# A hybrid decoder layer on 8 cores: a second residual tile, the next chunk's LayerNorm prologue placed inside the FFN, and one weight slot less

## The reference

```
x = layer_norm(x)
q, k, v, c_val, c_gate = split(x @ w_in)
att = rms_norm(causal differential attention(q, k, v))          # 4 heads
c = silu(group_norm(causal_conv31(c_val * sigmoid(c_gate)))) @ w_pw + b_pw
x = layer_norm(ALPHA * x + concat(att, c) @ w_o)                 # LN1
x = layer_norm(ALPHA * x + cross_attention(x, mem) @ w_o_mem)    # LN2
h = silu(x @ w_gate) * (x @ w_up)                                # d_ff = 2816
x = layer_norm(ALPHA * x + h @ w_down)                           # LN3, output
```

## Time and profile before

| | |
|---|---|
| runs before | 6143.0, 6189.2 and 6359.51 us; median 6189.2 |
| profiled execution | 6132.52 us, span of its slowest core 6130.7 us |
| spans of the 8 cores | 6099.5 to 6130.7 us |
| mean granted TensorE clock | 0.807 to 0.810 of full speed |
| busy: TensorE, DVE, ACT | 66%, 38%, 39% of the span |
| one chunk of the second phase | some 394 us, eight times |

### The profile page before, as it was taken

One profiled execution on the slowest core, in us unless ns is written; L12 is line 12 of the kernel. 1 busy time (PEld: TensorE's weight loads), 2 busy tenths in 40 slices (PEclk: granted clock), 3 DMA queues, 4 the chain that ended last, 5 costly groups with the idle time before them and its releaser, 6 DMA issues.

```text
span 6130.7 us, 75261 instructions; the slowest of 8 cores (6099.5 to 6130.7 us)
## 1 busy us (share of the span) xinstructions
PE 4025.9 (66%) x24208; PEld 2004.2 (33%) x24208; DVE 2327.8 (38%) x5354; ACT 2396.5 (39%) x3180; POOL 196.2 (3%) x230
## 2 busy tenths in 40 slices
PE   4566776776666767777467575684666846658467
PEld 2333433443333333344223232231322322223223
DVE  3433333122543331321353453535534345244453
ACT  2455665765445556567231221312213113132131
POOL 0000000000000000000001000010000000000000
PEclk8778888887777778888679787796877977879778
DMA  3111111011111100100538255382473743826536
GB/s 84 42 42 42 42 42 42 1 25 42 69 42 42 42 28 15 42 15 1 103 55 130 56 94 112 55 124 65 83 127 57 106 89 62 148 42 102 108 55 107
DMA packets 273353, 395.66 MB, mean 65 GB/s; under 512 B 6964, under 2 KB 230732, under 8 KB 272972
## 3 DMA queue, kind: packets, MB, share of 16 engines
q0 software_dynamic: 226848, 217.07, 23.9%
q1 hardware_dynamic: 46124, 173.77, 8.1%
HBM read 591.09 MB, written 16.78 MB: 99 GB/s over the span
## 4 chain that ended last, share of the span: by engine, by line
PE 41%; ACT 20%; DVE 19%; issue 9%; DMA 9%; DVEq 1%; ACTq 0%; SPq 0%; POOL 0%; POOLq 0%
PE PS L394 39%; ACT U L595 10%; ACT U L388 3%; DVE U L338 3%; DVE U L336 2%; DMA U<-w_up 2%; ACT U L361 2%; DMA U<-xown 2%; DMA U<-xkv 2%; DMA U<-w_down 2%; DVE U L880 2%; PE PS L378 1%; DVEq L148 1%; DVE U L357 1%; DVE U L340 1%
## 5 line engine op out<-in xcount | busy, mean ns | idle before, releaser
L394 PE MATMUL PS<-U 128*128 128x129 bf16 (+4 forms) x21696 | 3720.1, 327 | 780.9 <-ACT U L595 232.7
L394 PEld LDWEIGHTS PS<-U 128*128 128x128 bf16 (+2 forms) x21696 | 1811.2, 104 | 2653.8 <-issue 1719.2
L595 ACT ACTIVATE U<-PS,U 128x1024 bf16<-128x1024 f32 (+3 forms) x1152 | 1163.0, 1041 | 225.5 <-PE PS L394 155.7
L378 PE MATMUL PS<-U 128*128 128x128 bf16 x2368 | 307.7, 269 | 805.8 <-ACT U L361 654.3
L587 DVE TENSOR_TENSOR PS<-PS,U 128x128 f32<-128x128 f32 x512 | 137.9, 296 | 1250.3 <-PE PS L394 1249.1
L378 PEld LDWEIGHTS PS<-U 128*128 128x128 bf16 x2368 | 188.1, 115 | 924.3 <-issue 922.3
L388 ACT ACTIVATE U<-PS,U 128x512 bf16<-128x512 bf16 (+1 forms) x512 | 369.9, 755 | 203.9 <-PE PS L378 199.6
L479 PE MATMUL PS<-U 128*128 128x128 bf16 x128 | 34.0, 265 | 475.9 <-DVE U L477 475.9
L740 DVE SCALAR_TENSOR_TENSOR U<-U,PS 128x512 f32<-128x512 f32 x192 | 132.1, 688 | 481.6 <-PE PS L394 481.6
L908 ACT ACTIVATE U<-PS 128x512 f32<-128x512 f32 x176 | 105.1, 597 | 490.3 <-PE PS L394 431.5
L336 DVE BATCH_NORM_STATS2 U<-U 128x6 f32<-128x512 f32 x328 | 214.5, 654 | 189.6 <-DMA U<-xown 106.7
(11 more groups left out here) (80 smaller groups left out, 1821.9 us busy)
## 6 DMA issues: line engine op xcount, KB each, us to landing
U<-xkv SPq DMA_DIRECT2D x32, 2048.0 KB, 7.6
U<-xown SPq DMA_DIRECT2D x24, 2048.0 KB, 7.7
U<-w_gate POOLq DMA_DIRECT2D x40, 1024.0 KB, 10.4
U<-w_up POOLq DMA_DIRECT2D x40, 1024.0 KB, 13.8
U<-rowp SPq DMA_DIRECT2D x64, 512.0 KB, 6.5
U<-w_down POOLq DMA_DIRECT2D x32, 1024.0 KB, 16.3
U<-w_in POOLq DMA_DIRECT2D x16, 1024.0 KB, 13.9
U<-w_o POOLq DMA_DIRECT2D x16, 1024.0 KB, 8.7
```

Source lines behind the costliest of these rows:

```text
L378: P.op(PE, lambda e, j=j, dt=dt, tpb=tpb, j0=j0, zt=zt: e.transpose(out=tpb[:, (j - j0) * 128:(j - j0 + 1) * 128], in_=zt[:, j, dt * 128:( ...
L394: P.op(PE, lambda e: e.matmul(out, lhsT=lhsT, rhs=rhs, start=start, stop=stop, skip_group_check=True), reads=reads, writes=writes)
L595: P.op(ACT, lambda e, Sps=Sps, pti=pti, q0=q0, bcol=bcol: e.activation(out=Pt[pti][:, :, q0:512], in_=Sps.rearrange("p (a b) -> p a b", a= ...
```

## The change

It does four things.
- `R2`, a second residual tile of 16 KB per partition, is added, and chunks alternate between `R` and `R2`. Room is made by `NSLOT` 3 instead of 4 (8 KB per partition), by laying `xh32` over the two `sg` tiles (`sgx`), and by laying `memT` into `hT`.
- The prologue becomes a function (`prologue`), called once ahead of the loop for chunk 0, and for chunk ck + 1 between the last gate/up product of chunk ck and its `residual_mm` with w_down. It ends with the z step (`x_z`). The halo load now writes the `sg` buffers.
- Gains and biases of LN0 (`x_affine(0, 1)`) stay at the head of the chunk, with their two row loads. The z step of `ln_full` and of LN3 runs for all four blocks first, and then gains and biases block by block.
- A barrier is added after the memory projection.

```
-        NSLOT = 4
+        NSLOT = 3
...
-        xh32 = AR.alloc([128, D], F32)
-        b_xh = Buf()
+        R2 = AR.alloc([128, 4, D], F32)
+        b_R2 = [Buf() for _ in range(4)]
...
-        sg = [AR.alloc([128, 512], F32) for _ in range(2)]
+        sgx = AR.alloc([128, D], F32)
+        sg = [sgx[:, 0:512], sgx[:, 512:1024]]
         b_sg = [Buf(), Buf()]
+        xh32 = sgx
...
-        memT = AR.alloc([128, 8, MEM], BF16)
+        memT = hT[:, 0:4, :].rearrange("p a b -> p (a b)").rearrange("p (a b) -> p a b", a=8)
...
         ckp('mem')
+        P.barrier()
...
+        def x_z(nb=4):
+            for j in range(nb):
+                P.op(DVE, lambda e, j=j, R=R: e.tensor_scalar(out=R[:, j, :], in0=R[:, j, :], scalar1=lnt[:, j, 1:2],
+                                                              scalar2=lnt[:, j, 2:3], op0=ALU.mult, op1=ALU.add),
+                     reads=[b_lnt], writes=[b_R[j]])
+
+        def x_affine(grow, brow):
+            sg_ = load_row_bc(grow)
+            sb_ = load_row_bc(brow)
+            for j in range(4):
+                P.op(DVE, lambda e, j=j, sg_=sg_, R=R: e.tensor_tensor(out=R[:, j, :], in0=R[:, j, :], in1=gbt[sg_],
+                                                                       op=ALU.mult),
+                     reads=[b_gbt[sg_]], writes=[b_R[j]])
+                P.op(DVE, lambda e, j=j, sb_=sb_, R=R: e.tensor_tensor(out=R[:, j, :], in0=R[:, j, :], in1=gbt[sb_],
+                                                                       op=ALU.add),
+                     reads=[b_gbt[sb_]], writes=[b_R[j]])
...
+        def prologue(ck_):
+            load_x(xown[ck_ * 512:(ck_ + 1) * 512, :], 4)
+            dma(SP, xh32, xhalo[ck_ * 128:(ck_ + 1) * 128, :], "xh", writes=[b_sg[0], b_sg[1]])
+            srcs = [(R[:, j, :], b_R[j]) for j in range(4)] + [(xh32, (b_sg[0], b_sg[1]))]
             ln_stats(srcs, 5)
             ln_apply_bf(srcs)
             ln_transposes(5, C_G0, C_B0, (6, 7))
...
+            x_z()
+
+        dg_idx = [0]
+
+        Rs = [(R, b_R), (R2, b_R2)]
+        prologue(0)
+        for ck in range(NQT):
+            R, b_R = Rs[ck % 2]
+            x_affine(0, 1)
...
+            if ck + 1 < NQT:
+                Rsave = (R, b_R)
+                R, b_R = Rs[(ck + 1) % 2]
+                prologue(ck + 1)
+                R, b_R = Rsave
             residual_mm(2, lambda f: hT[:, f, :], b_hT, w_down, NFT)
             ckp('ffn')
             srcs = [(R[:, j, :], b_R[j]) for j in range(4)]
             ln_stats(srcs, 4)
...
+            x_z()
+            x_affine(6, 7)
```

More of the change, by code:

```diff
@@ L333, in ln_stats @@
         def ln_stats(srcs, nb, part="all"):
+            srcs = [(a_, list(b_) if isinstance(b_, (tuple, list)) else [b_]) for a_, b_ in srcs]
             if part in ("all", "dve"):
@@ L336, in ln_stats @@
                 P.op(DVE, lambda e, j=j, src=src: e.bn_stats(out=stt[:, j, 0, :], in_=src[:, 0:512]),
-                     reads=[sb_], writes=[b_st[j]])
+                     reads=sb_, writes=[b_st[j]])
                 P.op(DVE, lambda e, j=j, src=src: e.bn_stats(out=stt[:, j, 1, :], in_=src[:, 512:1024]),
-                     reads=[sb_], writes=[b_st[j]])
+                     reads=sb_, writes=[b_st[j]])
                 P.op(DVE, lambda e, j=j: e.bn_aggr(out=mv[:, j, :], in_=stt[:, j, :, :]),
@@ L358, in ln_apply_bf @@
                         out=zt[:, j, :], in0=src, scalar1=lnt[:, j, 1:2], scalar2=lnt[:, j, 2:3],
-                        op0=ALU.mult, op1=ALU.add), reads=[sb_, b_lnt], writes=[zbufs[j]])
+                        op0=ALU.mult, op1=ALU.add), reads=sb_ + [b_lnt], writes=[zbufs[j]])
                     continue
@@ L362, in ln_apply_bf @@
                                                                       bias=lnt[:, j, 2:3], scale=lnt[:, j, 1:2]),
-                     reads=[sb_, b_lnt], writes=[zbufs[j]])
+                     reads=sb_ + [b_lnt], writes=[zbufs[j]])
         def ln_transposes(nb, gcol, bcol, tbanks, zt=None, zbufs=None, evac="mix"):
@@ L689, in build_program @@
         for j in range(2):
-            P.op(ACT, lambda e, j=j: e.activation(out=zb[:, j, :], in_=R[:, j, :], func=AF.Copy),
+            P.op(ACT, lambda e, j=j, R=R: e.activation(out=zb[:, j, :], in_=R[:, j, :], func=AF.Copy),
                  reads=[b_R[j]], writes=[b_zb[j]])
@@ L739, in residual_mm @@
                         if si == nslab - 1:
-                            P.op(DVE, lambda e, tb=tb, r=r, nh=nh: e.scalar_tensor_tensor(
+                            P.op(DVE, lambda e, tb=tb, r=r, nh=nh, R=R: e.scalar_tensor_tensor(
                                 out=R[:, tb, nh * 512:(nh + 1) * 512], in0=R[:, tb, nh * 512:(nh + 1) * 512],
@@ L743, in residual_mm, with ln_full @@
                                 reads=[b_R[tb], REGB[r]], writes=[b_R[tb]])
-        def ln_full(gcol, bcol, grow, brow, want_x=True):
+        def x_z(nb=4):
[13 more added lines that the diff above has]
+                     reads=[b_gbt[sb_]], writes=[b_R[j]])
+        def ln_full(gcol, bcol, grow, brow):
             srcs = [(R[:, j, :], b_R[j]) for j in range(4)]
@@ L749, in ln_full @@
             ln_transposes(4, gcol, bcol, (6, 7))
[L750 to L769, removed]
+            x_z()
+            x_affine(grow, brow)
+        def prologue(ck_):
+            load_x(xown[ck_ * 512:(ck_ + 1) * 512, :], 4)
+            dma(SP, xh32, xhalo[ck_ * 128:(ck_ + 1) * 128, :], "xh", writes=[b_sg[0], b_sg[1]])
+            srcs = [(R[:, j, :], b_R[j]) for j in range(4)] + [(xh32, (b_sg[0], b_sg[1]))]
             ln_stats(srcs, 5)
```

## The result

The changed kernel is slower: ratio 1.0386 to the kernel before, 95% interval 1.0303 to 1.047. Its median is 6466.4 us over 9 runs (lowest 6373.3), against 6224.9 over 10 runs of before (lowest 6132.9). The profiled one took 6373.3 us, with a span of 6371.8 against 6130.7 before: 241 us more.

What follows compares the result with a forecast made beforehand. The prediction saw no single bound but a series of stages, each with its own limit. Its terms, 292 + 191 - 220 + 8 = +271 us, put the profiled 6132.5 us at 6404; it forecast 6435, range 6300 to 6590.

Steps and rivals of the forecast that it cites:

- (a): FFN gate/up: with three slots TensorE waits for up slabs and restarts at lower clock; 36.5 us per chunk, 292 us.
- rival 1: FFN weight slots: three suffice and (a) is nil; -21 us, about 6120 to 6170; chance 9%.
- rival 2: TensorE stalls: the clock stays up over gaps of 5 us; +182 us, 6325 on the lowest run; chance 12%.
- rival 3: FFN weight loads: transfers collide more, slabs land in 13.8 us; +216 us more, about 6640; chance 7%.
- rival 5: rival 1 and Rival 4 at once, the overlap is free; -177 us, 5966; chance 3%.
- (b): Between gate/up and down projection: the inserted prologue delays the down projection 27.3 us, seven times, 191 us.
- Rival 4: Between gate/up and down: the prologue is hidden, 5 us instead of 27.3; +115 us, 6260; chance 4%.
- (c): Chunk boundary: the second GLU column group's matmuls start 31.5 us sooner, seven times, 220 us saved.
- (d): Start of the second phase: the x load now follows the barrier; 8 us more, once.

Runs made afterwards that it cites:

- three-slot kernel: The kernel before with NSLOT 3 instead of 4, nothing else: 6468.4 us profiled, ratio 1.0422 to the kernel before.
- four-slot one: The changed kernel with NSLOT 4 instead of 3, the rest kept: lowest execution 6066.5 us, ratio 0.9785 to the kernel before.
- filled waits: The changed kernel with 24 unused matmuls ahead of the first up run of each FFN group from 1 on: 6305.5 to 6308.6 us, ratio 1.0101.
- early front: The changed kernel with four slots, own halo tile, prologue loads and statistics before FFN group 2, ACT part before group 4: 5953.3 and 5955.2 us.
- late gains: The early front with LN0's gains, biases and their two row loads moved after the convolution: 5802.7 to 5810.9 us, ratio 0.9477 to the kernel before.

## Why the prediction was right

The direction, the time and the size held: 6435 predicted for a median of 6466, and +271 us predicted for +241 between the profiled executions. The second comparison is the one that tests the mechanism: the sum gives 6404 for the profiled execution, which took 6373.3, so it is 31 us too high. That 6435 lies 31 us below the median instead depends on which executions came out long, and is luck. By its own steps:

(a) Three slots. Predicted 28.1 us of wait and 9.5 us of clock in each chunk, less 1 us, 36.5 in all; measured 38.5 (117.5 - 79.0). The waits are 231.4 us over 40, 5.8 us each on the mean; the step had 5.8 for four groups of a chunk and 4.9 for the first. A landing of 8.4 us was assumed, 8.3 is the median. Clock: the remainder, 38.5 - (231.4 - 7.8) / 8 = 10.5 us, so 2.1 us per wait where the step took 1.9. The three-slot kernel and the four-slot one show that this part is the slot's and carries the sign, and the filled waits that at least 1.6 of the 2.1 us per wait are clock. The size of the clock's part is in some degree luck: it was read from waits of the convolution and of the boundary. In the convolution's the mean clock is 0.54, and here it is 0.97 and the fall comes only at the wait's end. Rivals 1, 2 and 3 fall with it, and rival 5, which needs rival 1.

(b) The prologue in between. Predicted 27.3 us. Measured: the gap grew from 2.7 to 26.3 us, 23.6, and the down projection takes 2.0 us longer from its first matmul to the last residual add (40.9 against 38.9, here too the restart): 25.6. I had taken 8.7 us until the halo's statistics can start; it was 6.9 (from 4599.77 + 0.69 to 4607.40). Halo and statistics of the four blocks finished almost together: in seven chunks DVE waited 5.7 us in all for the halo, whose median landing was 7.2 us. So the step came out close to the lower end that it named. From there to the down projection it was 18.6 us, as taken (17.25 + 1.3). The early front shows what the 26.3 us were made of: 17 of them were order on DVE, halo and ACT together, which no run takes apart, and 9.3 are transposes. Rival 4 falls for this kernel, but the early front shows that most of its gain was to be had.

(c) The boundary. Predicted 31.5 us saved, measured 33.7 (75.8 - 42.1). Most of the missing piece is one I had in my own account in part (b): the table load for 1/std (1.28 us) is paid once in the prologue and no longer at LN3. Another 0.8 us goes because LN3 now runs z for all four blocks first (12.8 us for z, gains and biases instead of 13.6), a part of the change for which the prediction has no term. The wait for rows was 10.0 us, predicted 10.2. That gains and their rows were what is late next was tested by the late gains: 20.6 us each (40.05 to 19.40), near the 10.2 us of rows and 9.9 us of work in the step.

(d) The start of the phase. Here the step failed, in sign: "the load follows the barrier ... 8 us more". Measured from the issue of the memory load to the first GLU matmul: 2932.30 to 3002.15 is 69.9 us, against 2935.58 to 3011.52, 75.9 us, before. 6 us less. The new start, x load and first GLU matmul:

```profile
2967.53 0.37 SPq L302 DMA_DIRECT2D U<-xown  x1
...
3002.15 6.37 PE L396 MATMUL PS<-U 128*128 128x512 bf16 x32
```

From x load to GLU it is 34.6 us, near the 31.9 that I took. But the memory projection in front became shorter, some 17 us, because nothing else was being loaded. The view of w_kv_mem (who waited, landing min/median/max), first before, then after:

```profile
  PE PS L394: 18.4, 3
...
DMA to landing us min/median/max: 12.0/33.7/42.5
```

```profile
  PE PS L396: 3.8, 2
...
DMA to landing us min/median/max: 10.2/13.3/20.1
```

With x, halo, rows and w_in behind the barrier, the four slabs land in 13.3 us instead of 33.7 (medians). The changed kernel also has a slot less, so its last slab is issued later. With the slots held equal the landing still falls by the barrier: 33.7 to 19.7 us with four slots, 27.6 to 13.3 with three. From the first transpose to the last matmul the projection takes 43.8 us in the kernel before, 40.7 with three slots and no barrier, 26.6 in the changed kernel and 25.2 with barrier and four slots. So it is the barrier. I had counted what the barrier delays and not what it takes out of the way.

The sum: 8 x 38.5 + 7 x 25.6 - 7 x 33.7 - 6 = 245 us, against 241 measured. Of the 30 us between prediction and result, 15 are (c), 14 are (d) and 12 are (b), less 16 of (a) that went the other way; the remaining 4 are not attributed. Two figures of the prediction do not add up and change nothing: 4551.9 + 9 is 4560.9 and not 4561.5, and rival 3 comes to about 6630 on the lowest run and not 6640.

## What to carry to other kernels

Before a buffer is paid with a slot of another ring, write down for that ring which reader releases each slot and how much work is left from there to first use: here 3.5 us of work stood against a landing of 8.3 us, and one line cost more (308 us) than the shorter boundaries brought (7 x 33.7 = 236 us). Work that is moved "below" another stage overlaps only engine by engine: look at what stands ahead of it in every in-order queue, and cut it so that each engine's piece falls where that engine is idle. After a wait has been removed, ask which instruction is next in the same queue; here moving one vector step and its loads behind the convolution was worth 150 us (5953.3 to 5802.7), nearly as much as the double buffer with its prologue cut in three (6126.8, the lowest execution of the kernel before in that session, to 5953.3).

## What the runs showed of the hardware

In these waits the clock's fall is late: in a wait of 5.6 us the mean granted clock is still 0.97, and the loss comes in the matmuls after it (0.90 over 15.5 us). It is not so in every wait: in the convolution's, of about the same length, the mean is 0.54. Both cost more than their own time, and matmuls whose result nobody reads bought 65 us here by keeping the clock at or near 1.00 (1.00 in the stretch shown).

The Trainium skill (TensorE: Matmul & The Clock Gate, HAM oscillation — how this bites in real kernels) has the cost recur at every DMA wait of a loop. The trace agrees: each of the four full runs of 64 matmuls behind a wait took 15.5 to 16.9 us instead of 13.9.

Loads that overlap delay one another more than I had reckoned with: with four slots, the four w_kv_mem slabs had a median landing of 33.7 us with 3.5 MB of other loads and two w_in slabs beside them, and 19.7 us with those kept away. With three slots, where the fourth slab is issued later, it was 27.6 and 13.3 us.
